# Expert stage of a hybrid backbone step: gate pieces first, the hidden product in halves, transposes in between

## What is computed

```python
gate, idx = lax.top_k(aff.T, cap)
xs = xf[idx]
hid = silu(einsum('ecd,edf->ecf', xs, w_gate)) * einsum('ecd,edf->ecf', xs, w_up)
ye = einsum('ecf,efd->ecd', hid, w_down) * gate[..., None]
y = zeros_like(xf).at[idx.reshape(-1)].add(ye.reshape(-1, shp[-1]))
```

## Time and profile before

| | |
|---|---|
| median of three executions | 3357.63 us (3355.92 to 3358.09) |
| profiled execution | 3360.81 us |
| span of its trace | 3359.0 us |
| TensorE matmuls busy | 3028.8 us, 90% |
| VectorE busy | 1953.7 us, 58% |
| ScalarE busy | 1628.9 us, 48% |
| transfers | 684.70 MB, mean 204 GB/s |

### The profile page before, as it was taken

How to read it: one execution, slowest core, us unless ns; L and a number is a source line. 1 busy time by engine, 2 the same in 40 slices (tenths; PEclk the granted TensorE clock), 3 DMA queues, 4 the chain that set the end, 5 groups by cost and what they waited for, 6 DMA issues and landing times.

```text
span 3359.0 us, 38431 instructions
## 1 busy us (share of the span) xinstructions
PE 3028.8 (90%) x14213; PEld 2176.1 (65%) x14213; DVE 1953.7 (58%) x2038; ACT 1628.9 (48%) x1950; POOL 215.9 (6%) x183
## 2 busy tenths in 40 slices
PE   5899777899878899999999996899999999999993
PEld 1798333789645687878887883566666666666662
DVE  0443354443466444444444546788888788888884
ACT  2243232433345443443443342676666666766663
POOL 0000000000000200000000001011111111111100
PEclk7899778899999999999999998899999999999996
DMA  9522245122122322222234228999999999999994
GB/s 399 194 75 75 85 166 176 63 68 75 54 77 92 98 76 84 83 77 88 68 137 162 75 105 328 393 371 352 356 360 359 358 336 353 355 350 346 360 362 164
DMA packets 136081, 684.70 MB, mean 204 GB/s; under 512 B 13876, under 2 KB 13956, under 8 KB 66108
## 3 DMA queue, kind: packets, MB, share of 16 engines
q1 hardware_dynamic: 121920, 608.21, 48.1%
q0 software_dynamic: 12000, 74.89, 6.9%
q10 hardware_dynamic: 2064, 0.26, 0.1%
HBM read 651.78 MB, written 31.60 MB: 203 GB/s over the span
## 4 chain that ended last, share of the span: by engine, by line
PE 67%; DVE 7%; ACT 3%; issue 3%; DMA 2%; SPq 0%; POOL 0%; DVEq 0%; ACTq 0%; POOLq 0%
PE ps L717 30%; PE ps L1043 19%; PE ps L1060 12%; PE ps L734 2%; PE ps L741 1%; ACT ar L1224 1%; DMA hT<-w_exp_gate 1%; DVE soft L1540 1%; DVE ar L1538 1%; DVE ar L1555 1%; DVE ar L1678 1%; PE ps L979 1%; PE ps L1049 1%; ACT ar L1319 0%; DMA hT<-w_exp_down 0%
## 5 line engine op out<-in xcount | busy, mean ns | idle before, releaser
L717 PE MATMUL ps<-split_weights,split_tokens 128*128 128x512 f32 x5040 | 1160.8, 393 | 23.2 <-DVE split_tokens L416 11.3
L717 PEld LDWEIGHTS ps<-split_weights,split_tokens 128*128 128x128 f32 x5040 | 953.2, 190 | 229.0 <-issue 20.9
L1043 PE MATMUL ps<-split_experts,split_xsT 128*80 128x512 f32 x3072 | 715.2, 394 | 10.7 <-DVE split_experts L1668 10.7
L413 DVE TENSOR_TENSOR split_weights<-ring,split_weights 128x512 fp32r<-128x512 f32 x400 | 277.7, 694 | 749.9 <-ACT split_tokens L410 741.5
L409 ACT ACTIVATE split_weights<-ring 128x512 fp32r<-128x512 f32 x400 | 252.7, 632 | 831.6 <-PE ps L717 669.0
L1043 PEld LDWEIGHTS ps<-split_experts,split_xsT 128*80 128x80 f32 x3072 | 456.2, 149 | 267.7 <-DVE split_experts L1668 14.2
L1668 DVE TENSOR_TENSOR split_experts<-hT,split_experts 128x2048 fp32r<-128x2048 f32 x240 | 548.6, 2291 | 115.7 <-ACT split_experts L1309 115.7
L1309 ACT ACTIVATE split_experts<-hT 128x2048 fp32r<-128x2048 f32 x240 | 460.6, 1919 | 187.2 <-PE ps L1043 109.3
L1060 PE MATMUL ps<-split_experts,split_hidT 128*80 128x512 f32 x1536 | 391.2, 420 | 0.0
L1060 PEld LDWEIGHTS ps<-split_experts,split_hidT 128*80 128x80 f32 x1536 | 245.1, 161 | 139.7 <-issue 29.2
L416 DVE TENSOR_TENSOR split_tokens<-hT,split_tokens 128x640 fp32r<-128x640 f32 x320 | 263.2, 823 | 0.0
(11 more groups left out here) (257 smaller groups left out, 1888.3 us busy)
## 6 DMA issues: line engine op xcount, KB each, us to landing
ring<-w_mod SPq DMA_DIRECT2D x96, 1024.0 KB, 7.1
hT<-w_exp_gate SPq DMA_DIRECT2D x96, 1024.0 KB, 5.0
hT<-w_exp_down SPq DMA_DIRECT2D x80, 1024.0 KB, 9.4
ring<-w_in SPq DMA_DIRECT2D x68, 1024.0 KB, 5.1
hT<-w_exp_up SPq DMA_DIRECT2D x64, 1024.0 KB, 4.8
ar<-w_exp_up SPq DMA_DIRECT2D x32, 1024.0 KB, 6.6
ring<-w_exp_gate SPq DMA_DIRECT2D x32, 1024.0 KB, 10.0
ring<-w_exp_up SPq DMA_DIRECT2D x32, 1024.0 KB, 9.8
```

The lines of the kernel that those rows point to most:

```text
L413: a = self.eng.tensor_tensor(spW[:, s, 1, :], raw, spW[:, s, 0, :].bitcast(F32), ALU.subtract)
L717: mm = pe.matmul(ps[:, b, :], spX[:, s, x, b * P:(b + 1) * P], spW[:, s, w, :], start=(k == 0 and x == w), stop=(k == n_k - 1 and x == 1))
L1043: mm = pe.matmul(ps[0:CAP, 2 * up + n, :], xsT[:, x, k, :], spE[:, s, w, col:col + BANK], start=(k == 0 and x == w), stop=(k == KT - 1 and ...
```

## The change

Five things change, all in the expert stage.

1. The loads of an expert come as eight gate pieces, then eight up pieces, then eight down pieces. Rows of the weights are assigned to partitions in another way, so that each piece is a contiguous megabyte in memory; the transposes take the columns of `xs` and `hid` in the matching order.
2. Silu of the gate sums runs after ScalarE's split of piece 12; it waits for the eight gate pieces only.
3. The last up piece is done left half first, with a semaphore (`up_half`) behind it; the product with the up sums is made in two halves of 512 columns.
4. TensorE's order behind piece 15 is: four hidden transposes, twelve of the next rows, four hidden, the first down piece, the last four of the next rows. The transposed rows of `xs` go to banks 0 to 2, the hidden ones to banks 2 and 3.
5. The copies of the hidden blocks and of the next rows are cut to fit: two copies of four hidden blocks, and the copy of the next rows in a first part of twelve blocks and a second of four, with splits of pieces 18 to 20 between them.

```diff
-    w_eg = T["w_exp_gate"][0].rearrange("e (p k) n -> e p k n", p=P)
-    w_eu = T["w_exp_up"][0].rearrange("e (p k) n -> e p k n", p=P)
-    w_ed = T["w_exp_down"][0].rearrange("e (p k) n -> e p k n", p=P)
+    w_eg = T["w_exp_gate"][0].rearrange("e (g p k) n -> e g p k n", p=P, k=2)
+    w_eu = T["w_exp_up"][0].rearrange("e (g p k) n -> e g p k n", p=P, k=2)
+    w_ed = T["w_exp_down"][0].rearrange("e (k p) n -> e p k n", p=P)
...
-        xs_parts = parts((0, 2, 0, 6), (6, 3, 0, 6), (12, 1, 2, 4))
-        hid_parts = parts((0, 0, 0, 6), (6, 1, 0, 2))
+        xs_parts = parts((0, 0, 0, 6), (6, 1, 0, 6), (12, 2, 0, 4))
+        hid_parts = parts((0, 2, 0, 4), (4, 3, 0, 4))
...
-                    expert(2 * j, w_eg[ds(e, 1), :, 2 * j:2 * j + 2, :].squeeze(0), k2)
-                    expert(2 * j + 1, w_eu[ds(e, 1), :, 2 * j:2 * j + 2, :].squeeze(0), k2)
+                    expert(j, w_eg[ds(e, 1), j, :, :, :].squeeze(0), k2)
+                for j in range(8):
+                    expert(8 + j, w_eu[ds(e, 1), j, :, :, :].squeeze(0), k2)
...
+                    if j < 15:
+                        gate_up(j, (0, 1), (0, 1)).then_inc(piece_used, 1)
+                    else:
+                        gate_up(j, (0,), (0, 1)).then_inc(up_half, 1)
+                        gate_up(j, (1,), (0, 1)).then_inc(piece_used, 1)
+                pe.wait_ge(hd_r, 2 * e + 1)
+                hid_transposes(0)
+                pe.wait_ge(hd_s, e + 1)
                 pe.wait_ge(xs_ld, e * 16 + 32)
-                xs_transposes(e + 1)
-                pe.wait_ge(hd_cp, e + 1)
+                xs_transposes(0, 12, xs_first)
+                pe.wait_ge(hd_r, 2 * e + 2)
+                hid_transposes(1)
                 pe.wait_ge(ye_r, e + 1)
                 for k in range(FT):
                     s = (16 + k) % SP
                     pe.wait_ge(piece_ready, e * EXP_G + (P_EXP + 16 + k + 1))
+                    if k % 4 == 0:
+                        pe.wait_ge(hd_cp, 2 * e + (k // 4 + 1))
...
+                    if k == 0:
+                        xs_transposes(12, KT, xs_tr)
...
             def expert_act(e, last):
-                split_expert(e, AHEAD, 19)
-                act.wait_ge(piece_used, e * EXP_G + (SP + P_EXP + 16))
+                split_expert(e, AHEAD, 13)
+                act.wait_ge(piece_used, e * EXP_G + (SP + P_EXP + 8))
                 act.activation(hid[0:CAP, :], ps[0:CAP, 0:2, :].rearrange("p b n -> p (b n)"), ACT.Silu).then_inc(hd_s, 1)
...
+                split_expert(e, 13, 19)
+                copy_hid(e, 0)
+                copy_hid(e, 1)
+                act.wait_ge(xs_first, e + 2)
+                copy_xs(0, 2)
+                split_expert(e, 19, 20)
                 act.wait_ge(xs_tr, e + 2)
-                copy_xs()
-                split_expert(e, 19, EXP_G)
+                copy_xs(2, 3)
+                split_expert(e, 20, EXP_G)
...
             def expert_dve(e, last):
-                low_expert(e, AHEAD, 19)
+                low_expert(e, AHEAD, 18)
                 dve.wait_ge(hd_s, e + 1)
...
+                dve.wait_ge(up_half, e + 1)
+                hid_product(0)
+                dve.wait_ge(piece_used, e * EXP_G + (SP + P_EXP + 16))
+                hid_product(1)
+                low_hid(e, 0)
+                low_expert(e, 18, 19)
+                low_hid(e, 1)
+                dve.wait_ge(xs_h, 2 * e + 3)
+                low_xs(0, 2)
+                low_expert(e, 19, 20)
+                dve.wait_ge(xs_h, 2 * e + 4)
+                low_xs(2, 3).then_inc(xs_l, 1)
+                low_expert(e, 20, EXP_G)
```

More of the change, by code:

```diff
@@ L1009, in _, with xs_transposes, hid_transposes @@
             pe.transpose(ps[0:CAP, 7, NE:2 * NE], vals[0:NE, :], ident[0:NE, 0:NE]).then_inc(tk_tr, 1)
[L1011 to L1023, removed]
+            def xs_transposes(lo, hi, done):
+                v = xs[0:CAP, :].rearrange("r (g p k) -> r g k p", g=8, k=2)
+                for k in range(lo, hi):
+                    mm = pe.transpose(ps[:, k // 6, (k % 6) * CAP:(k % 6 + 1) * CAP], v[:, k // 2, k % 2, :],
+                                      ident[0:CAP, 0:CAP])
+                mm.then_inc(done, 1)
+            def hid_transposes(half):
+                for k in range(4):
+                    col = (4 * half + k) * P
+                    mm = pe.transpose(ps[:, 2 + half, k * CAP:(k + 1) * CAP], hid[0:CAP, col:col + P], ident[0:CAP, 0:CAP])
+                mm.then_inc(hd_tr, 1)
             mod_granules(3)
@@ L1027, in _ @@
             pe.wait_ge(af_cp, 1)
-            xs_transposes()
+            xs_transposes(0, 12, xs_first)
+            xs_transposes(12, KT, xs_tr)
             mod_granules(3)
@@ L1031, in _, with gate_up @@
             with pe.Fori(0, NE) as e:
+                def gate_up(j, n, kks):
+                    bank, k0, s = 2 * (j // 8), 2 * (j % 8), j % SP
+                    for kk in kks:
+                        k = k0 + kk
+                        for x, w in ((0, 0), (0, 1), (1, 0)):
+                            for i in n:
+                                col = kk * FF + i * BANK
+                                mm = pe.matmul(ps[0:CAP, bank + i, :], xsT[:, x, k, :], spE[:, s, w, col:col + BANK],
+                                               start=(k == 0 and x == w), stop=(k == KT - 1 and x == 1))
+                    return mm
                 pe.wait_ge(xs_l, e + 1)
                 for j in range(16):
-                    g, up = j // 2, j % 2
-                    s = j % SP
                     pe.wait_ge(piece_ready, e * EXP_G + (P_EXP + j + 1))
[L1038 to L1050, removed]
+                    if j < 15:
[6 more added lines that the diff above has]
+                pe.wait_ge(hd_s, e + 1)
                 pe.wait_ge(xs_ld, e * 16 + 32)
-                xs_transposes(e + 1)
-                pe.wait_ge(hd_cp, e + 1)
+                xs_transposes(0, 12, xs_first)
+                pe.wait_ge(hd_r, 2 * e + 2)
+                hid_transposes(1)
                 pe.wait_ge(ye_r, e + 1)
@@ L1296, in _, with copy_xs, copy_hid @@
             act.activation(aff[:, 0], aff[:, 0], ACT.Exp).then_inc(af_e, 1)
-            def copy_xs():
-                for dst, src in xs_parts:
+            def copy_xs(lo, hi):
+                for dst, src in xs_parts[lo:hi]:
                     a = act.activation(xsT[:, 0, dst:dst + src.shape[1], :], src, ACT.Copy)
                 a.then_inc(xs_h, 1)
+            def copy_hid(e, half):
+                act.wait_ge(hd_tr, 2 * e + (half + 1))
+                dst, src = hid_parts[half]
+                act.activation(hidT[:, 0, dst:dst + 4, :], src, ACT.Copy).then_inc(hd_h, 1)
             def split_expert(e, lo, hi):
@@ L1655, in _, with low_xs @@
             dve.tensor_copy(gateT[0:CAP, :], ps[0:CAP, 7, NE:2 * NE]).then_inc(tk_cp, 1)
-            def low_xs():
-                for dst, src in xs_parts:
+            def low_xs(lo, hi):
+                for dst, src in xs_parts[lo:hi]:
                     n = src.shape[1]
@@ L1660, in low_xs, with hid_product, low_hid @@
                                           ALU.subtract)
-                a.then_inc(xs_l, 1)
+                return a
+            def hid_product(half):
+                cols = slice(half * BANK, (half + 1) * BANK)
+                dve.tensor_tensor(hid[0:CAP, cols], hid[0:CAP, cols], ps[0:CAP, 2 + half, :], ALU.mult).then_inc(hd_r, 1)
+            def low_hid(e, half):
+                dve.wait_ge(hd_h, 2 * e + (half + 1))
+                dst, src = hid_parts[half]
+                dve.tensor_tensor(hidT[:, 1, dst:dst + 4, :], src, hidT[:, 0, dst:dst + 4, :].bitcast(F32),
+                                  ALU.subtract).then_inc(hd_cp, 1)
             def low_expert(e, lo, hi):
```

23 lines of the change are left out of this document (5 added, 18 removed).

## The result

The changed kernel takes 3256.1 us (median) against 3357.86 for the kernel before on the same chip: a ratio of 0.9694, 95% interval 0.968 to 0.9709. One of its four executions took 10208.42 us; it counts in the median and not in the ratio, and the other three took 3251.85, 3253.8 and 3258.4. The profiled execution took 3258.4 us with a span of 3256.6 (before 3359.0).

The account below looks back on a forecast made before the run. Bound: TensorE in the expert stage, idle in the up-to-down turn, then slowed by its clock. Turn 58 us plus clock 33, less 2.4 of issue gaps, gain 88 us: 3270 us, range 3260 to 3296 (78%).

Parts of the forecast that it names:

- the price of a transpose: Turn from up to down product: 24 transposes at 0.12 us take 2.9 us, so the turn falls from 6.50, saving 58 us.
- gate and up products: Expert stage: gate before up keeps the same instructions and shapes, so no change in time.
- issue gaps: TensorE's stream: three more waits cost 0.15 us per turn, 2.4 us in all.
- the clock: TensorE's clock stays at 1.00 through the turn, so sixteen down products get 33 us back.
- Silu off the path, product in halves: Turn: 2.30 us of silu and table load leave the path; product halves run from −1.2 and 0 to 0.75 us.
- The second rival: Turn: first product half comes late behind a VectorE split, TensorE idles up to 2.3 us each, 3307 us; 6%.
- ScalarE's lateness hidden: Among the up pieces: silu makes ScalarE late by 2.30 us, hidden under a cover of 3.8 us.
- The rival that transposes are too thin: Turn: transposes are thinner work, the clock falls anyway and 33 us stay lost, 3300 to 3303 us; 8%.
- its forecast's own spread: Whole kernel: 3262 to 3284 us, from 0.112 us transposes without gaps to 1 us unseen waiting per turn.
- Transfers: Expert-stage loads: 69.3 us period asks 384 GB/s, hidden; rival that they already bound, 3358 us, 5%.
- The rule weighed in the prediction: Trainium skill, DMA page: about 358 GB/s per core, so 74.3 us per expert, gain 13 us, 3345 us.
- Contiguous loads slower: Expert-stage loads: contiguous megabytes load memory unevenly; at 340 GB/s the period is 78.2 us, 3408 us; 3%.

Follow-up runs that it names:

- e2: e1 with gate pieces ahead of up pieces and silu behind the split of piece 12, product still one instruction: 3341.57 us, ratio 0.995 to the kernel before.
- e3: e2 with VectorE's hidden product ahead of its split of piece 18: 3324.55 us, ratio 0.9904 to the kernel before.
- e7: Changed kernel with silu made five times in a row in each expert: 3306.48 us, ratio 0.9857 to the kernel before.
- e8: Changed kernel with hidden transposes taking every fourth column of their half again, down rows loaded to match: 3264.65 us, ratio 0.9728 to the kernel before.
- e6: Changed kernel with the turn's twelve transposes of the next rows made twice: 3279.86 us, ratio 0.9774 to the kernel before.
- e11: Changed kernel unaltered, run once more: 3259.23 us, ratio 0.971 to the kernel before.
- e1: Kernel before with only the new assignment of weight rows to partitions, all orders as before: 3351.69 us, ratio 0.9985 to the kernel before.
- e10: Changed kernel with three more unused one-megabyte loads in each expert: 3337.59 us, ratio 0.9938 to the kernel before.
- e9: Changed kernel with one more unused one-megabyte load in each expert: 3260.1 us, ratio 0.9705 to the kernel before.
- e4: Changed kernel with all sixteen transposes of the next rows behind the first down piece: 3274.47 us, ratio 0.975 to the kernel before.

## Why the prediction came out as it did

Right in direction, mechanism and order of size; 14 us short, and outside its range. The step that failed is the price of a transpose; it is 6.8 of the 14 us, and with it alone put right the forecast's 3270 would have been 3263. Scatter ahead of the stage (3.0), gate and up products (2.6) and issue gaps (2.4) add to it; the first expert's turn and the clock take back 0.5 each. By its steps:

- **Silu off the path, product in halves.** Right. VectorE's first half runs at −1.27 us for 0.68 (predicted −1.2 and 0.69), the second ends at 0.72 (predicted 0.75). e2 and e3 show what the prediction did not say: silu alone gives next to nothing, since the split of piece 18 is next, and the product's place behind that split decides. What its halving adds was not tried apart. The second rival, a late first half, comes true in the first expert's turn only (0.93 us).
- **ScalarE's lateness hidden.** Right; the cover is 3.4 us (e7), 3.8 were predicted.
- **The price of a transpose.** This step failed. It took 0.12 us for all 24 and priced the new order of rows within a tile at nothing, "same instructions, same shapes". The columns are not the same: the eight hidden transposes now read adjacent columns, 0.067 us each. Sixteen at 0.12 and eight at 0.067 are 2.46 us in place of 2.88; the measured turn is 2.42. That is 6.8 us in sum, and e8 gives most of it back. The earlier trace rows was read as the other end, 0.112: it is of adjacent columns, but of 128 rows where these have 80.
- **Issue gaps.** 2.4 us were taken off for three more waits; none shows.
- **Clock.** 33 us predicted, 32.5 measured. The rival that transposes are too thin is refuted by after itself, and for a longer stretch by e6 beside e11's first turn.
- **Gate and up products.** Predicted unchanged; each expert's take 0.17 us less, 2.6 us in sum. It comes with e2 (order of pieces, place of silu) and not with e1. Why a matmul takes 0.2295 and not 0.2304 us there was not tried.
- **Ahead of the stage.** 3.0 us, by chance as far as the runs show. They, and the changed kernel's two medians of 3256.1 and 3259.2, show that 3 us of scatter belonged into the range, which stopped 2 us below its forecast's own spread. That spread was also added up wrong by 2 us at either end: 0.112 us for a transpose and no gaps give 3264, and 1 us more in each turn gives 3286.
- **Transfers.** Right: 388 GB/s where 384 were forecast. The room was estimated as 28.3 MB in 69.3 us, 408 GB/s; e10 stops at 403. The rule weighed in the prediction, a share of 358 GB/s for a core, doesn't bind here: e9 loads 402 in the mean. The Trainium skill says so itself on another page than the one cited: HBM Reference, Specifications (TRN2), gives that figure for two cores that stream at once and about 425 for one alone. The trace agrees: 426 and 434 in single stretches, 403 over whole experts.
- **Contiguous loads slower.** Refuted by e1, by after's 388 GB/s and by e9's 402.

## What to carry to other kernels

When a wait on a path is taken away, look at what is queued ahead of the next step on its engine: here silu's removal was worth almost nothing until the product moved ahead of a split. An idle gap between products can be paid twice, once as idle time and once in the slower clock behind it, so filling it with work that is due anyway can buy both. If a change rearranges memory, price its transposes by the column stride as well as by shape.

## What the runs showed of the hardware

- A transpose of 80 rows by 128 columns of 32-bit numbers costs 0.067 to 0.07 us with adjacent columns and 0.11 to 0.12 with a stride of two, four or more columns, at full clock. Over all of after, the weight load of one takes 138 to 166 ns for adjacent columns (hidden blocks) and 194 to 226 for every second (next rows).
- The granted clock stayed at 1.00 through 3.4 us of transposes alone (e6), through gaps of 0.49 and 0.15 us between them (e4), and through 1.68 us of idling between two dense products (e7); it fell to 0.50 behind gaps of 1.31 and 0.79 us with transposes between them (e3), and behind 2.83 (before). With one gap of about 0.9 us ahead of the transposes it fell in some turns (e11's first, e7's last) and held in others (after's first, e7's turn shown).
- One core's transfers, loads of a megabyte with one gather and one scatter in some 70 us, reached 402 GB/s (e9) and no more than 403 with two loads more (e10).
